# A two-layer decoder trunk on one core: attention queries ahead of the convolution's column tiles, and paged values and scores pulled forward by four loop items

## What is computed

```
hc, gc, gb, cq, ckv, kpe = split(rms(x) @ w_in)        # 3*512, 384, 256, 32 columns
up   = concat(conv_prev, gc * hc)                      # gated short convolution, 3 taps
y_conv = gb * (w0*up[t] + w1*up[t+1] + w2*up[t+2])
q    = rms(cq) @ w_uq                                  # 8 heads, 64 + 32 (rotary)
q_lat = q_nope @ w_uk
prompt: softmax(q k^T) v, causal, 8 heads, 4 blocks of 128 queries
sample: softmax over 16 cached pages + new rows, in the latent space of 256
y    = concat(y_conv, y_att) @ w_out
```

## Time and profile before

| | |
|---|---|
| three runs | 1526.95, 1529.85, 1532.02 us (median 1529.85) |
| profiled execution | 1531.82 us, span 1530.0 us |
| PE, DVE busy | 97%, 67% of the span |
| ACT, POOL busy | 18%, 7% |
| mean granted TensorE clock | 0.989 of full speed |
| median from issue to landing | key page 2.9 us, weight unit of 1 MB 4.8 us |

### The profile page before, as it was taken

The page is one execution under the profiler, slowest core; times in us unless marked ns, Lnnn a source line. Parts: engine busy times, 40 slices in busy tenths (PEclk is TensorE's granted clock), DMA queues, the critical chain, the costliest instruction groups (busy, mean ns, idle before and its releaser), DMA issues.

```text
span 1530.0 us, 18923 instructions
## 1 busy us (share of the span) xinstructions
PE 1479.8 (97%) x7084; PEld 1189.5 (78%) x7084; DVE 1018.7 (67%) x2068; ACT 269.4 (18%) x564; POOL 103.0 (7%) x114
## 2 busy tenths in 40 slices
PE   7999989899999999999999899999999999999996
PEld 6887735488888888888877778788888888888885
DVE  3363265868776676766865876877866767767845
ACT  4000034412101001001233321121001011011232
POOL 0002223400000000000200001300000000000100
PEclk9999999999999999999999999999999999999998
DMA  8205677712222222222203211222222222222201
GB/s 320 102 33 165 181 212 211 255 56 83 83 83 83 83 84 83 83 83 97 83 28 142 72 67 55 87 83 81 79 82 79 81 80 80 81 81 95 81 28 59
DMA packets 39470, 152.36 MB, mean 100 GB/s; under 512 B 6674, under 2 KB 19379, under 8 KB 26707
## 3 DMA queue, kind: packets, MB, share of 16 engines
q1 hardware_dynamic: 34258, 134.37, 25.4%
q0 software_dynamic: 5120, 16.78, 3.7%
HBM read 148.11 MB, written 3.02 MB: 99 GB/s over the span
## 4 chain that ended last, share of the span: by engine, by line
PE 90%; DVE 5%; DMA 2%; issue 1%; POOL 1%; SPq 0%; ACT 0%; DVEq 0%; POOLq 0%
PE psum L530 69%; PE psum L500 15%; PE psum L658 1%; DMA arena<-in_keys 1%; DMA ring<-in_weights 1%; PE psum L485 1%; DMA arena<-in_rows,vidx 1%; PE psum L764 1%; POOL arena L434 0%; PE psum L729 0%; PE psum L785 0%; PE psum L826 0%; DVE arena L1151 0%; PE psum L693 0%; PE psum L643 0%
## 5 line engine op out<-in xcount | busy, mean ns | idle before, releaser
L530 PE MATMUL psum<-arena 128*128 128x272 f32 x2016 | 478.9, 393 | 0.0
L530 PEld LDWEIGHTS psum<-arena 128*128 128x128 f32 x2016 | 383.0, 190 | 78.6
L1151 DVE TENSOR_TENSOR arena<-psum,arena 128x272 f32<-128x272 f32 x564 | 249.0, 441 | 248.5 <-PE psum L530 226.1
L530 PE MATMUL psum<-B,ring 128*128 128x272 f32 x736 | 184.7, 393 | 3.2 <-issue 1.8
L500 PE MATMUL psum<-A,ring 128*128 128x272 f32 x704 | 169.8, 403 | 9.0 <-DMA ring<-in_weights 7.8
L500 PEld LDWEIGHTS psum<-A,ring 128*128 128x128 f32 x704 | 136.8, 195 | 40.7 <-issue 11.8
L530 PE MATMUL psum<-arena,ring 128*128 128x272 f32 x672 | 167.7, 392 | 0.0
L530 PEld LDWEIGHTS psum<-B,ring 128*128 128x128 f32 x736 | 139.0, 190 | 32.6 <-issue 2.6
L530 PE MATMUL psum<-A,ring 128*128 128x272 f32 x608 | 152.6, 393 | 1.6 <-DVE A L1594 1.5
L530 PEld LDWEIGHTS psum<-arena,ring 128*128 128x128 f32 x672 | 127.4, 190 | 26.0
L530 PEld LDWEIGHTS psum<-A,ring 128*128 128x128 f32 x608 | 115.4, 190 | 26.0 <-DVE A L1594 2.0
(11 more groups left out here) (224 smaller groups left out, 1250.8 us busy)
## 6 DMA issues: line engine op xcount, KB each, us to landing
ring<-in_weights SPq DMA_DIRECT2D x98, 1024.0 KB, 4.8
arena<-in_keys SPq DMA_DIRECT2D x128, 144.0 KB, 2.9
arena<-in_attw SPq DMA_DIRECT2D x1, 3072.0 KB, 20.9
h<-in_xT SPq DMA_DIRECT2D x4, 544.0 KB, 7.8
out_yT<-A SPq DMA_DIRECT2D x8, 272.0 KB, 2.3
arena<-in_pemb SPq DMA_DIRECT2D x2, 544.0 KB, 5.8
ring<-in_weights SPq DMA_DIRECT2D x2, 512.0 KB, 6.8
arena<-in_bias SPq DMA_DIRECT2D x1, 640.0 KB, 8.5
```

What stands on the lines that cost most here:

```text
L530: end = pe.matmul(bank(g, n), lhs[:, c, :], x(c), start=c == 0, stop=c == 3)
L1151: ins = dve.tensor_tensor(out, bank(g, n), more, ALU.add)
```

## The change

Five edits in one:

1. Of the input projection, tiles 0 to 5 alone stand ahead of the queries: tiles 2 to 4, the query norm, tile 5, the key/value norm, and the query tiles. Convolution tiles 6, 7 and 8 move behind the latent queries. `score_pair(m)` follows tile 8+m, and tiles 16 and 17 follow `score_new(0)`, without scores. DVE and ACT follow this order, and the first group's exponentials run ahead of ACT's copies of the rotary key.
2. `up` moves to the buffers `sq` and `rbuf`, its two zero columns are written by DVE in each `conv` in place of POOL once. `conv(3)` moves behind DVE's copies of the keys and the turned probabilities.
3. Key and value tiles are interleaved with the `turn`s, then with `values_pair(0, 0)`, `score_pair(8)`, `values_pair(0, 1)` and `score_pair(9)`, which leave the loop.
4. The paged work in the loop stands four items earlier: first group's values and second group's scores in items 0 to 11, the group's end in 12 and 13, `turn`s in 14 to 18, the second group's values in items 20 to 27, its end in 28 and 29. Items 30 and 31 have no paged work.
5. SP issues `keys(2)` ahead of weight unit 8, and `keys(10)` and `keys(11)` ahead of the stores that wait for the convolution. POOL's waits for gathers 10 to 13 on `sc_full` fall by 4.

```diff
-T_COL = [0, 1, 3, 4, 5, 6, 7, 10, 11, 21, 22, 23, 24, 25, 26, 27, 28, 29]
-T_NQ, T_NKV = 8, 9
-T_UQ = 12
+T_COL = [0, 1, 3, 4, 5, 7, 18, 19, 20, 21, 22, 23, 24, 25, 26, 27, 28, 29]
+T_NQ, T_NKV = 6, 8
+T_UQ = 9
+LATE_VALUES = 20, 21, 22, 23, 24, 25, 26, 27
-        up = arena[:, 13760:13760 + 1124].rearrange("p (c t) -> p c t", c=2)
+        up = [x[:, :, :].rearrange("p c t -> p (c t)")[:, 0:562] for x in (sq, rbuf)]
...
SP
-            for u in range(4, 9):
+            for u in range(4, 8):
                 unit(u)
-            for m in range(2, 10):
+            keys(2)
+            unit(8)
+            for m in range(3, 10):
                 keys(m)
             sp.wait_ge(dve_x, 4)
             sp.dma_start(a["ckvT"]..., ckv)
+            keys(10)
+            keys(11)
             sp.wait_ge(conv_done, 1)
...
-            for m in range(10, 16):
+            for m in range(12, 16):
                 keys(m)
POOL
                 if 10 <= s < 14:
-                    pool.wait_ge(sc_full, 2 * s - 3)
+                    pool.wait_ge(sc_full, 2 * s - 7)
PE
-            for n in range(2, 7):
+            for n in range(2, 5):
                 in_ab(n)
+            pe.wait_ge(act_x, 3)
+            ones_tile(T_NQ, [qsq[:, i, :] for i in range(3)])
+            in_ab(5)
             pe.wait_ge(act_x, 5)
-            ones_tile(T_NQ, [qsq[:, i, :] for i in range(3)])
             ones_tile(T_NKV, [qsq[:, i, :] for i in range(3, 5)])
-            in_ab(7)
-            in_ab(8)
...
-            in_ab(9)
-            in_ab(10)
+            in_ab(6)
+            in_ab(7)
             pe.wait_ge(ql_ready, 2)
-            for m in range(7):
-                in_ab(11 + m)
+            for m in range(8):
+                in_ab(8 + m)
                 score_pair(m)
-            score_pair(7)
             score_new(0)
+            in_ab(16)
+            in_ab(17)
...
+            turn(0, 0)
+            turn(0, 1)
+            up_keys(0)
+            up_keys(1)
+            turn(0, 2)
+            turn(0, 3)
+            up_keys(2)
+            up_keys(3)
             turn(0, 4)
+            values_pair(0, 0)
+            up_values(0)
+            score_pair(8)
+            up_values(1)
+            values_pair(0, 1)
+            up_values(2)
+            score_pair(9)
+            up_values(3)
 
             def paged(n):
-                if n < 16:
+                if n < 12:
                     if n % 2 == 0:
-                        values_pair(0, n // 2)
+                        values_pair(0, 2 + n // 2)
                     else:
-                        score_pair(8 + n // 2)
-                elif n == 16:
+                        score_pair(10 + n // 2)
+                elif n == 12:
                     values_new(0)
                     score_new(1)
-                elif n == 17:
+                elif n == 13:
                     turn_out(0)
-                elif n < 23:
-                    if n == 19:
+                elif n < 19:
+                    if n == 15:
                         pe.wait_ge(ol_ready, 1)
-                    turn(1, n - 18)
-                elif 24 <= n < 32:
-                    values_pair(1, n - 24)
-                elif n == 32:
+                    turn(1, n - 14)
+                elif n in LATE_VALUES:
+                    values_pair(1, LATE_VALUES.index(n))
+                elif n == 28:
                     values_new(1)
-                elif n == 33:
+                elif n == 29:
                     turn_out(1)
DVE
-            for n in range(6):
-                scaled(n, cq[:, n, :] if n < 3 else ckv[:, n - 3, :] if n < 5 else kx)
-            scaled(6, stg[:, 0, :])
+            for n in range(5):
+                scaled(n, cq[:, n, :] if n < 3 else ckv[:, n - 3, :])
             norm_root(1, T_NQ, sq[:, 0, :], QR)
...
+            scaled(5, kx)
             norm_root(2, T_NKV, sq[:, 1, :], R)
...
-            conv(0)
-            for n in range(9, 18):
+            for n in range(6, 18):
                 scaled(n, stg[:, (n - 6) % 4, :])
-                if n % 3 == 2:
+                if n in (8, 11, 14):
                     conv(n // 3 - 2)
+                if n in (10, 12, 14):
+                    raw_max(0, (n - 10) // 2)
+                elif n == 15:
+                    raw_max(0, 3)
+                    soft_max(0)
+            turned(0, 0)
+            turned(0, 1)
+            keys_up(0)
+            keys_up(1)
+            turned(0, 2)
+            turned(0, 3)
+            keys_up(2)
+            keys_up(3)
+            turned(0, 4)
+            inverse(0)
+            conv(3)
+            dve.nop().then_inc(conv_done, 1)
             for i in range(4):
-                turned(0, i)
                 full(T_UV + i)
                 dve.tensor_copy(vtok[:, i, :], slot(T_UV + i)[:, 0, :]).then_inc(psum_free, 1)
+                if i == 1:
+                    raw_max(1, 0)
             dve.wait_ge(psum_free, T_OUTAB)
-            turned(0, 4)
-            inverse(0)
```

More of the change, by code:

```diff
@@ L707, in turn_out, with up_keys @@
                 last.then_inc(ot_full, 1)
-            in_ab(9)
-            in_ab(10)
+            in_ab(6)
+            in_ab(7)
             pe.wait_ge(ql_ready, 2)
-            for m in range(7):
-                in_ab(11 + m)
+            for m in range(8):
+                in_ab(8 + m)
                 score_pair(m)
-            score_pair(7)
             score_new(0)
-            for m in range(4):
+            in_ab(16)
+            in_ab(17)
+            def up_keys(m):
                 t = T_UK + m
@@ L723, in _, with up_values @@
                 last.then_inc(psum_full, 1)
-            for i in range(4):
-                turn(0, i)
+            def up_values(i):
                 t = T_UV + i
@@ L1025, in paged @@
             def paged(n):
-                if n < 16 and n % 4 == 3:
-                    raw(1, n // 4)
-                elif n == 16:
+                if n < 12 and n % 4 == 3:
+                    raw(1, n // 4 + 1)
+                elif n == 12:
                     out_scaled(0)
-                elif 17 <= n < 22:
-                    soft(1, n - 17)
-                elif n == 32:
+                elif 13 <= n < 18:
+                    soft(1, n - 13)
+                elif n == 28:
                     out_scaled(1)
@@ L1037, in _ @@
             act.wait_ge(ql_ready, 2)
+            for n in range(5):
+                soft(0, n)
             act.wait_ge(psum_full, T_COL[17] + 1)
@@ L1040, in _ @@
                 act.activation(K[64:96, hd, :], ssum[64:96, 0:TP], ACT.Copy).then_inc(k_rope, 1)
-            for n in range(5):
-                soft(0, n)
+            raw(1, 0)
             for n in range(NPR + 1):
@@ L1358, in ple @@
                     sum_sq(n, 7)
-            dve.wait_ge(consts, 2)
+            dve.wait_ge(consts, 1)
             for m in range(8):
@@ L1371, in conv @@
                 dve.wait_ge(psum_free, T_COL[3 * c + 8] + 1)
[L1372 removed]
+                link(dve.memset(up[b][:, 0:2], 0.0))
+                link(dve.tensor_tensor(up[b][:, 2:UPS], gc[:, 0:TP], hc[:, 0:TP], ALU.mult))
                 link(dve.tensor_copy(ups(c, 0, 2), stt[:, c, :, :]))
@@ L1420, in paged @@
             def paged(n):
-                if n < 16 and n % 4 == 3:
-                    raw_max(1, n // 4)
-                elif n == 16:
+                if n < 12 and n % 4 == 3:
+                    raw_max(1, n // 4 + 1)
+                elif n == 12:
                     soft_max(1)
-                elif n == 17:
+                elif n == 13:
                     out_turned(0)
-                elif 18 <= n < 23:
-                    if n == 18:
+                elif 14 <= n < 19:
+                    if n == 14:
                         dve.wait_ge(o_full, 1)
-                    turned(1, n - 18)
-                elif n == 23:
+                    turned(1, n - 14)
+                elif n == 19:
                     inverse(1)
@@ L1500, in _, with keys_up @@
             dve.nop().then_inc(ql_ready, 1)
-            conv(0)
-            for n in range(9, 18):
-                scaled(n, stg[:, (n - 6) % 4, :])
-                if n % 3 == 2:
[L1505 to L1511, removed]
+            def keys_up(c):
                 full(T_UK + c)
@@ L1515, in _ @@
                 dve.nop().then_inc(psum_free, 1)
+            for n in range(6, 18):
+                scaled(n, stg[:, (n - 6) % 4, :])
+                if n in (8, 11, 14):
+                    conv(n // 3 - 2)
+                if n in (10, 12, 14):
[15 more added lines that the diff above has]
+            dve.nop().then_inc(conv_done, 1)
             for i in range(4):
-                turned(0, i)
                 full(T_UV + i)
                 dve.tensor_copy(vtok[:, i, :], slot(T_UV + i)[:, 0, :]).then_inc(psum_free, 1)
+                if i == 1:
+                    raw_max(1, 0)
             dve.wait_ge(psum_free, T_OUTAB)
-            turned(0, 4)
-            inverse(0)
```

13 lines of the change are left out of this document (5 added, 8 removed).

## The result

The changed kernel takes 1542.56 us at the median of 9 runs (1535.56 to 1547.32), the kernel before 1530.08 (9 runs, 1526.95 to 1533.57): ratio 1.0073, 95% interval 1.0056 to 1.0089. By the ratio it is slower by some 11 us, where I forecast no change and a range up to 1535. The profiled execution took 1539.42 us with a span of 1537.6, against 1531.82 and 1530.0 before.

What follows compares the result with a forecast made beforehand. It took PE's own work as the bound, the end hanging on POOL's last gather: 291.5 plus 1.5 plus 15.5, less 0.1, is 308.4 against 308.0. So 1529.85 plus 0.4 gives 1530.3 us, range 1523.5 to 1535.

Steps and rivals of the forecast that it cites:

- the overlap: At the end of the tail, 0.1 us taken off the sum, giving the output projection's start at 308.4.
- Queries ahead: Query tiles ahead of tiles 6 to 8: PE waits for DVE at the fourth, +2.5 us, bounds 0 and 4.
- Key and value tiles: Interleaved stage before the loop: first value pair waits 1.8 us, conv(3) hidden; +0.8 us, bounds -1 and +4.
- Keys: Loop's key waits: 9.7 us lost before, 1.5 us of waits after, no clock drop; -8.2 us, wait bounds 0 and 5.
- The loop: Items after the start at 219.5: item 8 at 240.3, item 20 at 268.4, item 28 at 289.6 without the gather wait.
- POOL: Gather 8 starts at 242.1 and the issues end at 282.7 against 292.6 before, 9.9 us earlier.
- The landing: Gather 15 lands at 291.5 beside the weight units, a wait of 3.8 us in item 27; bounds 287 and 293.
- The tail: Items 28 to 33 to the output projection: 15.5 us, bare items giving PE idle time instead of speed.
- Rival 2: Half clock moves to the end: low clock behind item 27's gather wait, landing at 293, +4 to +6 us; chance 0.13.
- Rival 1: Last gather lands in time, some 4 us after its issue; -2 to -3 us; chance 0.17.
- three signs of being wrong: Keys waiting 4 us or more, last gather landing within 5 us of its issue, or tail 13 us or shorter.

Runs made afterwards that it cites:

- e1: Changed kernel with the four weight units of the output projection issued only once v_used is 16; ratio to the kernel before 1.0024.
- e4: Changed kernel with nine unread products of 512 columns, seven in item 27 and one each ahead of items 32 and 33; ratio to the kernel before 1.0060.
- e7: e1 again, the changed kernel with the four weight units held back until v_used is 16, in the third set; ratio to the kernel before 1.0036.
- e8: e7 with one unread product of 512 columns ahead of each of items 32 and 33; ratio to the kernel before 1.0021.
- c1: The changed kernel itself, timed and profiled again in the second set; ratio to the kernel before 1.0026.
- c2: The changed kernel itself, again, as the control of the third set; ratio to the kernel before 1.0083.
- e2: Changed kernel with the second group's values back in items 24 to 31, their end in 32 and 33; ratio to the kernel before 1.0008.
- e10: Changed kernel with score_pair(9) and values_pair(0, 1) exchanged, so key pair 11 is asked for 3.1 us earlier; ratio to the kernel before 1.0073.
- e14: e2 again, the changed kernel with the second group's values in items 24 to 31, with twelve executions; ratio to the kernel before 1.0025.
- e11: Changed kernel with convolution tile 6 ahead of the queries again, nothing else; ratio to the kernel before 1.0064.
- e9: Changed kernel with tile 6 ahead of the queries, second group's values in items 24 to 31, first value tile ahead of first value pair; ratio to before 0.9988.
- c0: The kernel before, unchanged, profiled beside its variants in the second set; 1549.78 us in the profiled execution, 1550.69 us as the set's measure.

## Why the prediction was wrong

The chain that I followed, last gather, landing, tail, was the one that set the end: it starts the output projection at 317.2, where I had 308.4. Of the 8.8 us, 4.1 are the landing (295.6 for 291.5), 1.0 the value pair behind it, which ran at half clock (2.5 us to item 28 for 1.5), 3.6 the tail (19.1 for 15.5), and the last 0.1 the overlap that I had taken off. So two terms of it were mis-sized; ahead of it I left the clock out of the queries' term and mis-sized the keys'.

- **Queries ahead, +2.5.** The wait was 2.64 us, at the fourth query tile, released by DVE, as worked out. But the clock fell behind it, and the eight tiles took 26.7 us in place of 22.16, +4.5. In four executions (e1, e4, e7, e8) the same wait left the clock at 1.00, and they took 25.0; in six (the changed kernel, c1, c2, e2, e10, e14) they took 26.4 to 28.1. The term is 2.9 to 5.9, by the execution; my upper bound was 4.
- **Key and value tiles, +0.8.** The first value pair waited 1.91 us (forecast 1.8), and item 0 came 39.8 us after the new scores, against 18.67 + 14.7 of the two moved tiles + 4.9 of the moved pairs = 38.3 before: +1.5. `conv(3)` stayed hidden.
- **Keys, 1.5 us of waits.** 2.5 in the first profile, 3.0 to 4.1 in seven of the ten profiles of the last three sets, with the low clock behind it in all seven: the gain of 8.2 was 7 in the first profile, and 4.7 less in c2 (items 0 to 8 took 26.0 us against 21.3). The wait before was made shorter at best, not taken away, and e10 shows that asking for one pair earlier hands it to the next.
- **The loop.** Item 8 at 242.2 (forecast 240.3), item 20 at 269.6 (268.4), item 27 at 288.6 behind gather 14's wait.
- **POOL.** Gather 8 started at 244.4 (242.1), the last issue ended at 284.8 (282.7). These 2 us are the slips of the stages ahead of it, the queries' first.
- **The landing: the first step that failed.** I put the landing of gather 15 at 291.5, from the bytes still open: a fixed 14.8 us behind the first weight unit. It was 295.6, 18.8 behind it. In that time the DMA moved 6.3 MB (18.8 us at 336 GB/s), not the 5.5 that I had counted, since POOL issues its gathers until 8 us behind the first unit; and the rate was below the 385 GB/s of the same stretch before, and far below the 411 that I had read off its end. My 5.5 MB at 411 GB/s would even be 13.4 us, not the 14 to 15 that I wrote. Why the rate was lower, and who had how much of it, the runs don't separate. That the weights beside the gathers are the cause of the wait is shown by e7, where the greatest landing falls from 11.8 to 4.9 us, no gather is waited for and 7 us come back. The wait was 8.4 us in two places, in place of 3.8 in one.
- **The tail: the second.** I gave it 15.5 us behind item 28 and said that the bare items give PE idle time. They do, and behind this idle time the clock stands at 1.2 GHz for the last products: 19.1 us. e8 shows the price of that: 2.1 us in the trace, 2.7 at the median. But even at 1.00 the tail took 16.8 us there and 16.2 in e4, so some 1 us of the miss is not the clock. Behind a gather's wait the low clock also takes the first products of the tail. Its price was not taken by itself, as e4 met no wait; it differs from one execution to the next, for the tail took 19.1 us in the first profile and in e10, no more than without a gather's wait (18.9, e7), and 21.6 and 21.3 in c2 and e11.

Rival 2, "the half clock moves to the end", is the nearest: the landing was late and the clock fell behind it. But it gave the landing 1.5 us more where it took 4.1, and it had the clock fall behind the gather's wait alone, not again behind the bare items, which is where e8 finds a price. It came out at 9.2 us in place of 4 to 6. I had given it 0.13. Rival 1 needed a landing within 4 us, and it took 11.8; the Trainium skill ("DMA: Bandwidth & Descriptors", SWDGE vs HWDGE vs iDMA) has the engines take turns between software and hardware queues. Whatever the turns are, the trace shows a gather's DMA three times as long on its way beside weight units as at the median. Of my three signs of being wrong (keys waiting 4 us, a landing within 5, a tail of 13 or less) none came in the first profile: two of them looked for an end sooner than forecast, and none for a later one at the landing or in the tail.

For the clock, the Trainium skill ("TensorE: Matmul & The Clock Gate", HAM oscillation) has work start cold again behind a wait for DMA. The traces agree: 0.50 behind the wait of 6.3 us. The same came behind a wait for DVE of 2.64 us, 0.65 in the first profile, but only in six of ten executions.

The two ways to cure the end say the same thing from both sides: hold the weights back (e7, 0.47% less) or leave the values where they were (e14, 0.5 to 0.6% less). What is left over the kernel before with the values late, 0.25% in e14, goes when the queries' and the turned copies' waits are cured too: e9 is level with before (0.9988, 0.9973 to 1.0003). What is left in e7, 0.36%, was not taken apart in the same way.

Open stays what the unnamed releases of the first two sets are, and how the low clock's share divides between its places in the median of many runs, since each profile shows one execution and they differ (item 28 at 298.2 in the first, 303.5 in c2).

## What to carry to other kernels

Work that is pulled forward pulls with it the loads that wait for it: here four weight units moved with the values and came down on the last gathers, and holding them back took off 0.47 of the control's 0.83%. Bare items at the end of a pipelined loop are not a gift when another engine sets their pace: they took as long as items with a value pair in them (18.9 us in e7, 17.7 in e14), and their last products ran at half the clock. Before moving work away from a chain, count what it was covering, and give each new wait a second price, that of the clock behind it: here the low clock followed a wait of 2.6 us in six of ten executions.

## What the runs showed of the hardware

- Behind a wait of 2.64 us the granted clock stood lower in six of ten executions (the eight query tiles then take 26.4 to 28.1 us) and at 1.00 in four (25.0), in kernels that are the same up to there.
- Two products that nothing reads, put where PE idled for DVE, kept the granted clock at 1.00 where it had been 0.50, and the stretch took 16.8 us in place of 18.9 (e8 against e7; 2.7 us at the median).
- An indirect DMA of 256 KB (a quarter of a gather) lands 3.7 us after its issue at the median, and up to 11.8 beside weight units, with the DMA at 414 to 419 GB/s in part of that time.
- The same chip ran the kernel before in 1551.27 us in the first set and in 1530.96 in the third. In c0, which took 1549.78 us, all of the difference lay ahead of the output projection (326.2 against 308.0), with stalls of ACT and DVE in the loop, and in that set the change cost 0.26% in place of 0.73.
